# A decoder trunk on one core: the gate's first token tile multiplies two of its four weight slots unsplit

## What is computed

```python
x = _layer_norm(ALPHA * x + ffn, ln_g[i, 1], ln_b[i, 1])
emb = p[i] @ ple_w_proj[i]
gate = jax.nn.sigmoid(x @ ple_w_gate[i] + ple_b_gate[i])     # ple_w_gate[i]: 1024 x 1024
x = x + gate * emb
```

## Time and profile before

| | us |
|---|---|
| median of 3 runs (1732.94 to 1736.3) | 1734.85 |
| the profiled execution | 1733.6 |
| its span, first to last instruction | 1731.8 |
| PE busy in it | 1649.8 |
| DVE busy in it | 721.4 |
| ACT busy in it | 468.5 |
| mean granted clock of PE, share of full speed | 0.979 |

### The profile page before, as it was taken

How to read it: one execution, slowest core, us unless ns; L and a number is a source line. 1 busy time by engine, 2 the same in 40 slices (tenths; PEclk the granted TensorE clock), 3 DMA queues, 4 the chain that set the end, 5 groups by cost and what they waited for, 6 DMA issues and landing times.

```text
span 1731.8 us, 18163 instructions
## 1 busy us (share of the span) xinstructions
PE 1649.8 (95%) x7678; PEld 990.8 (57%) x7688; DVE 721.4 (42%) x1060; ACT 468.5 (27%) x549; POOL 46.9 (3%) x47
## 2 busy tenths in 40 slices
PE   7999999979999999998799999999997999999996
PEld 6774343358777843433688778643434877434335
DVE  4572111284667711112756755411116657111126
ACT  4521111134443311111344342211102552111111
POOL 0000000100000000001010000000010000000010
PEclk9989999999999999999899999999999998999998
DMA  7489999945443899999344345999995558999990
GB/s 281 187 365 353 422 421 421 420 154 196 157 158 139 353 421 421 421 421 421 135 178 191 146 189 234 422 421 421 421 420 213 200 198 361 358 422 421 421 416 26
DMA packets 75147, 534.44 MB, mean 309 GB/s; under 512 B 8976, under 2 KB 9136, under 8 KB 10544
## 3 DMA queue, kind: packets, MB, share of 16 engines
q1 hardware_dynamic: 73728, 530.95, 75.4%
q0 software_dynamic: 1328, 2.21, 0.4%
HBM read 532.07 MB, written 1.05 MB: 308 GB/s over the span
## 4 chain that ended last, share of the span: by engine, by line
PE 82%; DVE 12%; DMA 2%; ACT 2%; issue 1%; SPq 0%; DVEq 0%; ACTq 0%
PE psum L890 37%; PE psum L531 10%; PE psum L532 10%; PE psum L533 10%; PE psum L882 4%; DVE w_lo L1378 4%; PE psum L900 3%; PE psum L542 3%; DMA raw<-in_experts 2%; ACT w_hi L1089 1%; PE psum L816 1%; PE psum L824 1%; DVE stats L1404 1%; DVE x L1446 1%; DVE x L1403 1%
## 5 line engine op out<-in xcount | busy, mean ns | idle before, releaser
L1378 DVE TENSOR_TENSOR w_lo<-raw,w_hi 128x2048 fp32r<-128x2048 f32 x120 | 271.1, 2287 | 158.1 <-ACT w_hi L1089 157.9
L531 PE MATMUL psum<-w_hi,xT_hi 128*128 128x512 f32 x704 | 282.9, 402 | 10.9 <-DVE w_lo L1378 6.5
L532 PE MATMUL psum<-w_lo,xT_hi 128*128 128x512 f32 x704 | 277.9, 395 | 0.0
L533 PE MATMUL psum<-w_hi,xT_lo 128*128 128x512 f32 x704 | 277.5, 394 | 0.0
L1089 ACT ACTIVATE w_hi<-raw 128x2048 fp32r<-128x2048 f32 x120 | 224.8, 1909 | 97.6 <-PE psum L533 92.4
L1378 DVE TENSOR_TENSOR work_r<-psum,work_r 128x512 fp32r<-128x512 f32 x84 | 56.7, 689 | 352.0 <-ACT work_r L1089 352.0
L1089 ACT ACTIVATE work<-psum 128x512 f32<-128x512 f32 x152 | 89.5, 599 | 413.2 <-PE psum L533 206.9
L890 PE MATMUL psum<-raw,xg 128*64 128x512 f32 x776 | 183.7, 598 | 0.0
L531 PEld LDWEIGHTS psum<-w_hi,xT_hi 128*128 128x128 f32 x704 | 134.8, 191 | 45.7 <-DVE xT_lo L1378 7.9
L533 PEld LDWEIGHTS psum<-w_hi,xT_lo 128*128 128x128 f32 x704 | 134.6, 191 | 28.9
L532 PEld LDWEIGHTS psum<-w_lo,xT_hi 128*128 128x128 f32 x704 | 134.8, 191 | 27.7 <-issue 0.2
(11 more groups left out here) (156 smaller groups left out, 1591.3 us busy)
## 6 DMA issues: line engine op xcount, KB each, us to landing
raw<-in_experts SPq DMA_DIRECT2D x144, 1024.0 KB, 13.5
raw<-in_slots SPq DMA_DIRECT2D x120, 1024.0 KB, 4.9
expert_work<-in_experts SPq DMA_DIRECT2D x96, 1024.0 KB, 15.2
expert_high<-in_experts SPq DMA_DIRECT2D x96, 1024.0 KB, 13.2
expert_bias<-in_experts SPq DMA_DIRECT2D x20, 1024.0 KB, 10.1
expert_norm<-in_experts SPq DMA_DIRECT2D x20, 1024.0 KB, 14.1
expert_y<-in_experts SPq DMA_DIRECT2D x4, 1024.0 KB, 15.3
expert_xg<-in_experts SPq DMA_DIRECT2D x4, 1024.0 KB, 8.5
```

Of the source, the lines that this page charges most:

```text
L531: mm(out, lhs[0], rhs[0], start=start, stop=False)
L532: mm(out, lhs[0], rhs[1], start=False, stop=False)
L533: return mm(out, lhs[1], rhs[0], start=False, stop=stop)
L1378: return tt(lo, whole, hi.bitcast(F), ALU.subtract)
```

## The change

- In the packed weights, the four gate slots of each layer are stored in the order 2, 3, 0, 1. They are loaded in the order of storage as before, and tile 1 uses them in that order.
- In tile 0 PE takes first the two slots stored last (rows 0 to 511 of the weight), straight from `raw`, and multiplies them in full precision with a full-precision copy of the first quad, `x_whole`, which ACT writes in place of the high copy. That is 4 multiplications per slot in place of 12. It then takes the slots stored first, in parts, as before.
- DVE makes no low quad for the first quad of tile 0. It splits the slots stored third and fourth not ahead of tile 1's rows and norm but after its low quads, and waits with each until PE has used it whole (`whole_used`).
- `keep_running` before the transposes of tile 0 goes from 10 to 16.

```diff
-                  by_rows(A["ple_w_proj"][layer]), by_rows(A["ple_w_gate"][layer])]
+                  by_rows(A["ple_w_proj"][layer]),
+                  np.roll(by_rows(A["ple_w_gate"][layer]), -WHOLE, 0)]
...
+        x_whole = xg[:, 0, :, :]
...
+        def whole_quads(k, t):
+            return WHOLE // 2 if k % 3 == 2 and t == 0 else 0
...
             def turned_quad(k, t, q):
-                pe.wait_ge(xt_ready, 4 * k + 2 * t + q + 1)
+                if q < whole_quads(k, t):
+                    pe.wait_ge(xt_hi, 4 * k + 2 * t + q + 1)
+                else:
+                    pe.wait_ge(xt_ready, low_parts(k, t, q))
...
+            def gate_slot(L, t, i):
+                s = i if t else (i + WHOLE) % 4
+                n, at = starts[L][2] + s, (s + WHOLE) % 4
+                whole = t == 0 and i < WHOLE
+                if i == 0 or whole or t == 0 and i == WHOLE or t and i == 2:
+                    turned_quad(3 * L + 2, t, at // 2)
+                if whole:
+                    pe.wait_ge(slot_full[n % RING], 16 * (n // RING + 1))
+                    w = quarters_of(raw[:, n % RING, :])
+                else:
+                    w = slot(n)
+                order = [(j, c) for j in range(2) for c in range(2)]
+                if i == 3:
+                    order = [(j, c) for c in range(2) for j in range(2)]
+                for j, c in order:
+                    bank, start, stop = psum[:, 2 * t + c, :], i + j == 0, i == 3 and j == 1
+                    if whole:
+                        last = mm(bank, x_whole[:, 2 * at + j, 0:P], w[:, 2 * j + c, :], start=start, stop=stop)
+                    else:
+                        last = product(bank, part(xv, ALL, 2 * at + j, bass.ts(t, P)), part(w, ALL, 2 * j + c), start, stop)
...
+                elif whole:
+                    last.then_inc(whole_used, 1)
...
-                keep_running(10, 5)
+                keep_running(16, 5)
                 transpose_tile(3 * L + 2, 0)
                 keep_running(3, 1)
...
                     if i == 3:
                         transpose_tile(3 * L + 2, 1)
-                    rows_slot(starts[L][2], 4, tiled(xv), 0, 0, i, ple_done)
+                    gate_slot(L, 0, i)
...
@@ ScalarE, save_tile
-                    copy(xT[0][:, 4 * q:4 * q + 4, t * P:(t + 1) * P], quad(4 + 2 * t + q)).then_inc(xt_hi, 1)
+                    turned_x = x_whole if q < whole_quads(k, t) else xT[0]
+                    copy(turned_x[:, 4 * q:4 * q + 4, t * P:(t + 1) * P], quad(4 + 2 * t + q)).then_inc(xt_hi, 1)
...
@@ VectorE, split_slot and save_tile
                 dve.wait_ge(hi_ready, n + 1)
+                for L in range(DEPTH):
+                    i = n - starts[L][2] - 2
+                    if 0 <= i < WHOLE:
+                        wait_whole(L, i)
...
-                for q in range(2):
+                for q in range(whole_quads(k, t), 2):
...
                 save_tile(3 * L + 2, 0)
-                split_behind(n_gate)
+                split_behind(n_gate - 2)
                 dve.wait_ge(ffn_done, T * L + 2)
                 for c in range(2):
                     add_rows(1, c)
                 layer_norm(1, 2 * L + 1)
                 save_tile(3 * L + 2, 1)
+                split_behind(n_gate)
```

More of the change, by code:

```diff
@@ L65 @@
 EARLY_K, LATE_K = 3, 9
+WHOLE = 2
 def expert_places():
@@ L282, in build @@
         x_half_ready, x_tile_ready, half_done = sem("x_half_ready"), sem("x_tile_ready"), sem("half_done")
+        whole_used = sem("whole_slots_used")
         put_half, general_done = sem("put_half"), sem("general_path_done")
@@ L368, in group_jobs, with low_parts @@
             return [(2 * q + i, t) for t in range(T) for i in range(2)]
+        def whole_quads(k, t):
+            return WHOLE // 2 if k % 3 == 2 and t == 0 else 0
+        def low_parts(k, t, q):
+            return 4 * k + 2 * t + q + 1 - WHOLE // 2 * (k // 3 + (k % 3 == 2))
         def quads(bank, n=4):
@@ L560, in turned_tile @@
             def turned_tile(k, t):
-                pe.wait_ge(xt_ready, 4 * k + 2 * (t + 1))
+                pe.wait_ge(xt_ready, low_parts(k, t, 1))
             def turned_quad(k, t, q):
-                pe.wait_ge(xt_ready, 4 * k + 2 * t + q + 1)
+                if q < whole_quads(k, t):
+                    pe.wait_ge(xt_hi, 4 * k + 2 * t + q + 1)
+                else:
+                    pe.wait_ge(xt_ready, low_parts(k, t, q))
             def turn_p(L):
@@ L652, in last_group @@
                     transpose_tile(3 * L + 1, 0)
+            def gate_slot(L, t, i):
[18 more added lines that the diff above has]
+                        last = product(bank, part(xv, ALL, 2 * at + j, bass.ts(t, P)), part(w, ALL, 2 * j + c), start, stop)
+                    if i == 3 and (j, c) == (1, 0):
+                        last.then_inc(half_done, 1)
+                if t:
+                    last.then_inc(weights_used, 1)
+                elif i == 3:
+                    last.then_inc(ple_done, 1)
+                elif whole:
+                    last.then_inc(whole_used, 1)
             def conv_mixer(L):
@@ L1070, in _ @@
                 for i in range(4):
-                    if i % 2 == 0:
-                        turned_quad(3 * L + 2, 0, i // 2)
                     if i == 3:
                         transpose_tile(3 * L + 2, 1)
-                    rows_slot(starts[L][2], 4, tiled(xv), 0, 0, i, ple_done)
+                    gate_slot(L, 0, i)
                 for i in range(4):
-                    if i % 2 == 0:
-                        turned_quad(3 * L + 2, 1, i // 2)
                     if i == 3 and L + 1 < DEPTH:
                         transpose_tile(3 * L + 3, 0)
-                    rows_slot(starts[L][2], 4, tiled(xv), 0, 1, i, ple_done)
+                    gate_slot(L, 1, i)
         @block.scalar
@@ L1381, in quad, with wait_whole @@
                 return psum[:, bank, :].rearrange("p (j n) -> p j n", j=4)
+            def wait_whole(L, i):
+                dve.wait_ge(whole_used, WHOLE * L + i + 1)
             def split_slot(n):
                 dve.wait_ge(hi_ready, n + 1)
+                for L in range(DEPTH):
+                    i = n - starts[L][2] - 2
+                    if 0 <= i < WHOLE:
+                        wait_whole(L, i)
                 rest(w_lo[:, n % RING, :], raw[:, n % RING, :], w_hi[:, n % HIGH, :]).then_inc(lo_ready, 1)
```

## The result

The changed kernel takes 1720.99 us (median of 4 runs, 1715.77 to 1722.19), the kernel before 1735.09 in the same comparison: a ratio of 0.9914, 95% interval 0.9891 to 0.9937. It is faster by 14 us, where 24.3 were forecast, and lies 3 us above the range. The four runs differ with the granted clock: 1715.77 us at 0.989, 1720.05 at 0.985, 1721.94 at 0.984 and 1722.19 at 0.983, so how often the clock falls changes from one execution of this kernel to the next. Its profiled execution took 1720.05 us (span 1718.2, mean granted clock 0.985 in place of 0.979), 13.6 us under that of before. Layers are counted from 0 to 3.

A forecast was written before the change was run, and what follows sets the result against it. DVE's order, not its total, bounds the gate stage. Layers 0 to 3 gain 6.4 + 4.3 + 6.4 + 7.2 = 24.3 us: profiled 1733.6 becomes 1709.3; that execution lay 1.25 under the median, so 1710.5, range 1705 to 1718 us.

The forecast's parts named there:

- Step 1: In tile 0 DVE drops one low quad and moves two splits behind the norm; T comes 5.01 us earlier.
- T: Start of PE's transposes of tile 1 in the gate stage; layer 0: 367.54 before, forecast 362.53.
- Step 2: In PE's tile 0, eight full-precision products replace 24 reduced ones, 1.40 us more per layer, ending 0.7 us ahead of T.
- New waits: I take 0: New small waits anywhere in the kernel: between 0 and 0.3 us each, counted as 0.
- Step 3: Behind T PE runs at full clock; T to token tile 1's first product takes 3.88 us, not 6.09: gain 2.21.
- The rival in which it falls all the same: Clock still falls around the shorter idle time ahead of T, so nothing is gained behind it: 1715.5 us, chance 0.14.
- Steps 4 and 5: Behind tile 1 DVE's moved splits, 2.20 us each, take back about 1.3 us; other pieces cost nothing except in layer 1.
- step 5: Other pieces: memory order, ScalarE, SyncE and GpSimd queues cost nothing, as their waits are for work that moves forward.
- Step 6: Layer 1's stall: six more warming products push the transposes about 1.5 us; 2.9 gained up to T, 4.3 in all.
- Step 7: Layer 3: same as layer 0, but no next layer takes anything back: 5.01 + 2.21 = 7.2 us.
- has little reason to move: Argument against the rival that layer 1's stall goes away: 1706.1 us, chance 0.13; stall entering another layer: 0.08.
- The slower one: Full-precision products in tile 0 run at 1.2 GHz, T 3.5 us later, 16.7 in all: 1751.5 us, chance 0.04.

The follow-up runs named there:

- the best version: Changed kernel with two slots unsplit in both token tiles, broadcast in VectorE's gap, ten warming products instead of sixteen: 1708.21 us, ratio 0.9843 to the kernel before.

## Why the prediction was off, point by point

*Step 1, DVE ahead of tile 1: right.* The lead won up to T is 4.98 and 5.00 us in layers 2 and 3, forecast 5.01. In layer 0 DVE won 4.99 too, by the norm of tile 1, but PE was late (next point).

*Step 2, PE in tile 0: right in size, and its slack was too thin once.* Counted as in step 2, the eight full-precision products take 6.87 us at full clock (from 832.56 in layer 1 to 839.66, where the records are back in step, less one pitch of 0.23), forecast 6.86. In layer 0 the clock was low from 352.30, at the end of the transposes, through the warming products and into the first of the eight. They then took 7.97 us of busy time where they have 7.03 in the other layers, and T came 0.93 us later than DVE would have allowed. "New waits: I take 0" and full clock here had only the row at 350.35 behind them. In the kernel before itself the same transposes of layer 3 stood behind the same idle time and ran at half clock:

```profile
1690.81 1.97 PE L542 MATMUL psum<-const,x 128*128 128x128 f32 x8 [3.07 <-DVE x L1453]
```

I read one layer and took it for all four.

*Step 3, the clock behind tile 1: right.* It is 1.00 from 364.40, and the kernel before with nothing but that gained 6.2 us. The rival in which it falls all the same is out at this place. The clock fell elsewhere, behind 2.20 us at the border, which no step had priced: 1.56 us in layers 0 and 1, as the run with warming products at the border shows.

*Steps 4 and 5, behind tile 1: here it failed.* The sum "splits until T + 7.06" took 2.20 us a split as on an idle machine, and step 5 gave GpSimd's queue a cost of nothing, since its waits "move forward". They do, and the broadcast moves with T, but the splits had been moved to the very place where it lands, 2.4 to 3.3 us after T in either kernel. T to the next layer took 18.66, 18.75 and 18.75 us where 16.87 were forecast, and 16.79 with the broadcast away. That is 1.8 to 1.9 us in each of three layers, some 5.5 of the 10.7 us that are missing. With 0.93 for PE in layer 0 and 3.1 for the two falls at the border 9.6 are accounted for.

The rest, 1.1 us, is what is left of larger pieces of both signs. The trace of after is 0.96 behind before it has met any gate; all ten other kernels without the twenty added products are behind there too, by 0.43 to 1.86, even the two that have the work of the kernel before up to there, so it is the one trace of before that is early. Between layers 2 and 3 2.18 us are lost, and the granted clock of after is 0.91 in the 20 us from 1406.98, where before, at the same distance from its layer's start, has 1.00. Between layers 1 and 2 it is the other way round (before 0.91 in the 20 us from 1003.75, after 1.00), and 0.76 us are won in spite of the fall at the border. No experiment here is on these falls.

*Step 6, layer 1: right up to T.* Up to T 2.96 us were won, forecast 2.9; what is missing in its stage is the broadcast.

*Step 7, layer 3: 7.7 for 7.2.* It has no next layer and so no broadcast, and its two splits took 4.48 us. In this layer the rest of the sum was sound: 5.00 us up to T for 5.01, and 2.7 behind it (21.1 us from T to the end, before 23.8) for 2.2.

*The rivals.* That the stall of layer 1 "has little reason to move" was wrong as a reason: it did stay in the changed kernel (5.41 us), but in eight of the twelve other kernels another layer's stall came, or this one went or shrank. *The slower one* didn't occur: with the clock low for a part of tile 0, PE lost 1.7 us, 0.7 of them covered by its slack, far from the 5.7 from which it would decide.

## What to carry to other kernels

When an instruction is moved, look at what every other engine does at its new place, and not only at who waits for it: a long VectorE instruction with both inputs in SBUF and a GpSimd broadcast did not run at the same time here, and that took back 1.8 to 1.9 us in each of three layers. Price a clock assumption from all the places in the trace that resemble it, since the same idle time was followed by a fall in one layer and not in the next. And if the profile puts idle time of TensorE down to "issue", try a few lengths of its program before judging any change by the total, for such a stall was worth up to 4.4 us here and moved with edits elsewhere.

## What was not expected of the hardware

- A split of 128 x 2048 beside a partition broadcast took 4.25 to 4.28 us in place of 2.28, or the broadcast 3.80 in place of 2.29: one waits for the other to end.
- The clock fell behind idle times of 2.20 and 2.19 us in layers 0 and 1 and not behind 2.19 in layer 2, and in the run with ten warming products behind none of the three, 2.18 to 2.19 us long. It fell behind 1.78 us in layer 0 (351.31) and not behind 1.77 in layer 2 (1316.03).
- Issue stalls of 1.8 to 5.4 us come in one or two of the four layers for the same work: layer 1 alone in both kernels; 0 and 2 with twenty products added ahead; layer 3 alone, with 1.83 us, in the best version.
